# Attention of a decoder step: four score banks in a ring, and the scores issued one job ahead

## What is computed

```python
def nsa_block(qp, qb):                       # per 128 queries, 8 heads, one shared K/V
    o_c, p_c = _sdpa(qb, kc, vc, dist_c, dist_c >= 0, slopes_a)      # 32 compressed keys
    ...
    o_s, _ = _sdpa(qb[:, :, None], kg, vg, dist_s, dist_s >= 0, slopes_a)  # selected blocks
o_w = _window_banded(qn, kw[:, w_buf:], vw[:, w_buf:], slopes_a)     # the last 512 keys
...
s = jnp.einsum('bqngmd,bknmd->bngmqk', qb, kd) * (HEAD_DIM ** -0.5)  # differential, 4 heads
p = _masked_softmax(s - slopes_b * dist, dist >= 0)
a = p[:, :, :, 0] - lam * p[:, :, :, 1]
o_b = jnp.einsum('bngqk,bknv->bqngv', a, vd)
```

## Time and profile before

| what | us |
|---|---|
| median of 3 runs (2192.03 to 2200.97) | 2200.1 |
| the profiled execution, its own time | 2199.43 |
| its span, first to last instruction | 2197.6 |
| TensorE busy | 2027.6 (92%) |
| VectorE busy | 1113.2 (51%) |
| ScalarE busy | 615.8 (28%) |

### The profile page before, as it was taken

The page is one execution under the profiler, slowest core; times in us unless marked ns, Lnnn a source line. Parts: engine busy times, 40 slices in busy tenths (PEclk is TensorE's granted clock), DMA queues, the critical chain, the costliest instruction groups (busy, mean ns, idle before and its releaser), DMA issues. The chain is left out here.

```text
span 2197.6 us, 33701 instructions
## 1 busy us (share of the span) xinstructions
PE 2027.6 (92%) x12602; PEld 1823.7 (83%) x12602; DVE 1113.2 (51%) x2445; ACT 615.8 (28%) x1220; POOL 116.4 (5%) x176
## 2 busy tenths in 40 slices
PE   6989999998996899999999879699999999999997
PEld 1338888878995788888988857499999999999996
DVE  0434333333235667677766634455555555555555
ACT  2123234321222566666660021210111101111012
POOL 1021100001300000002000000000000000000000
PEclk9989999999997799999999989899999999999998
DMA  9755554321101000000003440321120111111104
GB/s 321 264 186 171 163 152 145 113 83 49 49 1 62 1 1 1 1 1 1 1 25 120 125 147 36 96 58 29 57 57 29 57 41 45 57 29 57 38 0 154
DMA packets 132537, 166.43 MB, mean 76 GB/s; under 512 B 15851, under 2 KB 98635, under 8 KB 132372
## 3 DMA queue, kind: packets, MB, share of 16 engines
q1 hardware_dynamic: 117790, 134.75, 19.3%
q0 software_dynamic: 4832, 17.15, 2.5%
q10 hardware_dynamic: 9808, 13.11, 1.7%
HBM read 144.31 MB, written 22.77 MB: 76 GB/s over the span
## 5 line engine op out<-in xcount | busy, mean ns | idle before, releaser
L1642 DVE TENSOR_TENSOR late_x<-late_x,ffn_po 128x344 f32<-128x344 f32 x528 | 244.2, 509 | 116.4 <-PE ffn_po L1572 116.1
L1555 PE MATMUL ffn_pg<-late_words_hi,ffn_uhi 128*128 128x344 f32 x528 | 169.3, 321 | 14.7 <-DVE ffn_ulo L1606 14.7
L788 PE MATMUL nsa_out<-zs_z,nsa_probT 128*128 128x64 f32 (+1 forms) x1344 | 176.1, 277 | 5.8 <-DVE zs_z L944 5.6
L1516 ACT ACTIVATE ffn_sg<-ffn_pg 128x344 f32<-128x344 f32 x66 | 30.2, 458 | 534.2 <-PE ffn_pg L1555 534.2
L788 PEld LDWEIGHTS nsa_out<-zs_z,nsa_probT 128*128 128x128 f32 x1344 | 169.1, 198 | 7.8 <-DVE zs_z L944 7.7
L1572 PE MATMUL ffn_po<-ffn_a_hi,ffn_ohi 128*128 128x344 f32 x528 | 169.0, 320 | 0.2 <-DVE late_x L1642 0.2
L1555 PE MATMUL ffn_pg<-late_words_lo,ffn_uhi 128*128 128x344 f32 x528 | 169.1, 320 | 0.0
L1555 PE MATMUL ffn_pg<-late_words_hi,ffn_ulo 128*128 128x344 f32 x528 | 169.1, 320 | 0.0
L1572 PE MATMUL ffn_po<-ffn_a_hi,ffn_olo 128*128 128x344 f32 x528 | 168.9, 320 | 0.0
L1555 PE MATMUL ffn_pv<-late_words_hi,ffn_uhi 128*128 128x344 f32 x528 | 168.8, 320 | 0.0
L1555 PE MATMUL ffn_pv<-late_words_lo,ffn_uhi 128*128 128x344 f32 x528 | 168.7, 319 | 0.0
(11 more groups left out here) (452 smaller groups left out, 4524.0 us busy)
## 6 DMA issues: line engine op xcount, KB each, us to landing
mod_wr<-in_w_ada SPq DMA_DIRECT2D x12, 2048.0 KB, 8.9
ffn_raw_u<-in_w_ffn_in SPq DMA_DIRECT2D x44, 512.0 KB, 5.8
kin_kin<-in_cache_kv SPq DMA_DIRECT2D x64, 256.0 KB, 3.5
ffn_raw_o<-in_w_ffn_out SPq DMA_DIRECT2D x22, 512.0 KB, 3.6
gate_d<-dec_gate ACTq DMA_DIRECT2D x48, 172.0 KB, 2.4
late_x<-gate_d SPq DMA_DIRECT2D x8, 1032.0 KB, 5.2
dec_raw<-in_w_in POOLq DMA_DIRECT2D x16, 512.0 KB, 5.7
dec_vin<-in_cache_kv SPq DMA_DIRECT2D x64, 128.0 KB, 2.2
```

The lines of the kernel that those rows point to most:

```text
L788: mm = pe.matmul(out[jb.group % 2][:, jb.b, 0:w], probT[t % 2][:, q, :], g.z[:, jb.k0 // P + q, at:at + w], start=(q == 0), stop=(q == til ...
L1516: act.activation(sg[(j + c) % 2][:], pg[(j + c) % 2][:, 0:TCH], ACT.Silu).then_inc(silu_done, 1)
L1555: mm = pe.matmul(bank[b][:, 0:TCH], w[j][:, v * KD + k, :], h[:, k, tok], start=(k == 0 and q == 0), stop=(k == KD - 1 and q == 2))
L1642: dve.tensor_tensor(total[:, k, tok], total[:, k, tok], po[u % 4][:, 0:TCH], ALU.add).then_inc(o_read, 1)
```

## The change

The four score banks become one tensor with a ring: an item takes as many banks as its keys need (one for up to 512 columns, two for more; every other item one), the next free ones in order, and starts again at bank 0 where it would not fit at the end. For each item the list `earlier` holds the last item that used one of its banks, and TensorE waits for that one to be drained, not for the item two back. And on TensorE `follow(x - 1)` comes after the score of job x, where `follow(x)` came: the score of a job is issued ahead of the transposes of the job five back and the products of the job six back. The programs of ScalarE and VectorE keep their order; only the places they read are others.

```diff
+    BANK, BANKS = 512, 4
+    start, earlier, at_bank, holder = [], [], 0, [None] * BANKS
+    for n, (kind, x) in enumerate(items):
+        jb = jobs[x] if kind == "unit" else jobs[x[0]] if kind == "scores" else None
+        size = (jb.k1 - jb.k0 + BANK - 1) // BANK if jb else 1
+        if at_bank + size > BANKS:
+            at_bank = 0
+        held = [holder[b] for b in range(at_bank, at_bank + size) if holder[b] is not None]
+        start.append(at_bank * BANK)
+        earlier.append(max(held) if held else None)
+        for b in range(at_bank, at_bank + size):
+            holder[b] = n
+        at_bank = (at_bank + size) % BANKS
...
-        sc = [s.ps(f"sc{i}", [P, SEQ]) for i in range(2)]
+        sc = s.ps("sc", [P, BANKS * BANK])
...
                 for n, (kind, x) in enumerate(items):
-                    slot = n % 2
-                    if n >= 2:
-                        drained(n - 2)
+                    c0 = start[n]
+                    if earlier[n] is not None:
+                        drained(earlier[n])
...
                     if kind == "unit":
                         jb = jobs[x]
-                        score(slot, 0, (qhi[jb.head % 2], qlo[jb.head % 2]), jb.tile, jb.k0, jb.k1, g.kk[jb.b]).then_inc(sc_full, 1)
-                        follow(x)
+                        score(c0, (qhi[jb.head % 2], qlo[jb.head % 2]), jb.tile, jb.k0, jb.k1, g.kk[jb.b]).then_inc(sc_full, 1)
+                        follow(x - 1)
...
                         if m == 1:
-                            follow(t)
-                for t in range(NJ, NJ + LAG + 1):
+                            follow(t - 1)
+                for t in range(NJ - 1, NJ + LAG + 1):
                     follow(t)
```

More of the change, by code:

```diff
@@ L747, in _, with score @@
             def _(pe):
-                def score(slot, c0, q, i, k0, k1, keys):
+                def score(c0, q, i, k0, k1, keys):
                     for a, b in key_chunks(k1 - k0):
                         for n in range(2):
-                            mm = pe.matmul(sc[slot][:, c0 + a:c0 + b], q[n][:, i * P:(i + 1) * P], keys[:, k0 + a:k0 + b],
+                            mm = pe.matmul(sc[:, c0 + a:c0 + b], q[n][:, i * P:(i + 1) * P], keys[:, k0 + a:k0 + b],
                                            start=(n == 0), stop=(n == 1))
@@ L821, in _ @@
                         for t in range(4):
-                            mm = pe.transpose(sc[slot][:, t * P:(t + 1) * P], qd[:, 4 * half + t].rearrange("p a b -> p (a b)"), g.ident[:])
+                            mm = pe.transpose(sc[:, c0 + t * P:c0 + (t + 1) * P], qd[:, 4 * half + t].rearrange("p a b -> p (a b)"), g.ident[:])
                         mm.then_inc(q_ps, 1)
@@ L827, in _ @@
                         for t in range(4):
-                            mm = pe.transpose(sc[slot][:, t * P:(t + 1) * P], q2d[:, 4 * half + t, y % 2].rearrange("p a b -> p (a b)"), g.ident[:])
+                            mm = pe.transpose(sc[:, c0 + t * P:c0 + (t + 1) * P], q2d[:, 4 * half + t, y % 2].rearrange("p a b -> p (a b)"), g.ident[:])
                         mm.then_inc(q2_ps, 1)
@@ L832, in _ @@
                         for i in range(TT):
-                            mm = score(slot, 32 * i, (qhi[x % 2], qlo[x % 2]), i, 0, 32, g.kkc)
+                            mm = score(c0 + 32 * i, (qhi[x % 2], qlo[x % 2]), i, 0, 32, g.kkc)
                         mm.then_inc(sc_full, 1)
@@ L837, in _ @@
                         for half in range(2):
-                            mm = pe.transpose(sc[slot][:, half * P:(half + 1) * P],
+                            mm = pe.transpose(sc[:, c0 + half * P:c0 + (half + 1) * P],
                                               scmp[:, 4 * half:4 * half + 4, :].rearrange("p t n -> p (t n)"), g.ident[:])
@@ L843, in _ @@
                         for half in range(2):
-                            mm = pe.matmul(sc[slot][:, half * 4 * HD:(half + 1) * 4 * HD], pcT[:, half, :],
+                            mm = pe.matmul(sc[:, c0 + half * 4 * HD:c0 + (half + 1) * 4 * HD], pcT[:, half, :],
                                            g.vcb[:].rearrange("p a b -> p (a b)"), start=True, stop=True)
@@ L855, in _ @@
                             pe.wait_ge(q2_lo, 4 * jb.head + 2 * m + 2)
-                        score(slot, 0, (q2hi[m], q2lo[m]), jb.tile, 0, jb.k1, g.kk[2 + jb.head // 2 * 2 + m]).then_inc(sc_full, 1)
+                        score(c0, (q2hi[m], q2lo[m]), jb.tile, 0, jb.k1, g.kk[2 + jb.head // 2 * 2 + m]).then_inc(sc_full, 1)
                         if m == 1:
-                            follow(t)
-                for t in range(NJ, NJ + LAG + 1):
+                            follow(t - 1)
+                for t in range(NJ - 1, NJ + LAG + 1):
                     follow(t)
@@ L898, in _ @@
                         act.wait_ge(q_ps, 2 * h + half + 1)
-                        act.activation(qhi[h % 2][:, half * HALF:(half + 1) * HALF], sc[n % 2][:, 0:HALF], ACT.Copy).then_inc(q_hi, 1)
+                        act.activation(qhi[h % 2][:, half * HALF:(half + 1) * HALF], sc[:, start[n]:start[n] + HALF], ACT.Copy).then_inc(q_hi, 1)
                     if kind == "two queries":
@@ L902, in _ @@
                         act.wait_ge(q2_ps, 2 * y + half + 1)
-                        act.activation(q2hi[y % 2][:, half * HALF:(half + 1) * HALF], sc[n % 2][:, 0:HALF], ACT.Copy).then_inc(q2_hi, 1)
+                        act.activation(q2hi[y % 2][:, half * HALF:(half + 1) * HALF], sc[:, start[n]:start[n] + HALF], ACT.Copy).then_inc(q2_hi, 1)
                     if kind == "unit":
@@ L1003, in minimum @@
                     dve.wait_ge(sc_full, scored[n])
-                    dve.tensor_tensor_reduce(pr, sc[n % 2][:, 0:w], table[:, -w:], -1.0, 3e38, ALU.add, ALU.min, negmax).then_inc(biased, 1)
+                    dve.tensor_tensor_reduce(pr, sc[:, start[n]:start[n] + w], table[:, -w:], -1.0, 3e38, ALU.add, ALU.min, negmax).then_inc(biased, 1)
                 def close(t):
@@ L1026, in _ @@
                 for n, (kind, x) in enumerate(items):
-                    at_sc = sc[n % 2]
+                    at_sc = sc[:, start[n]:]
                     if kind == "queries":
```

## The result

The changed kernel takes 2268.6 us (median of 4 runs) against 2200.5 us: a ratio of 1.032, 95% interval 1.029 to 1.034. It is 68 us slower. The forecast had the sign right, 16 us of it, and a range that ended at 2240 us. All of the difference is in the attention stage: the last products, issued at 1143.67 us before, are issued at 1208.85 us now, 65 us later.

A forecast was written before the change was run, and what follows sets the result against it. TensorE was taken to bound the attention stage. New stalls of 44 us, counted as 33, less 10.2, 8 and 2, gave +13 us idle; with +3 us of clock on 2199.4 us that made 2216 us, range 2180 to 2240 us.

The forecast's parts named there:

- an unmoved `close(x)`: On VectorE, `close(x)` follows the minimum of x and waits for second-group transposes of x-4, now behind score x+1; 80 jobs.
- The overlap: TensorE's new stalls: each gives VectorE and ScalarE time for the next chain, so three quarters of 44 us count, 33 us.
- the neighbours: Score banks: 6 items wait for the one directly in front, in tile 4 and differential jobs; 7.4 us together.
- the queries: TensorE: 15 items wait for an item "queries" of the job directly before; 1.6 us each, 12 counted, 19 us.
- distance three: Score ring: 89 items wait for the item three back, asking for the same minimum as before.
- The 8 us taken off for the other waits: TensorE's waits for output buffer, evacuation and minimum, 11.5 us: 8 go, since scores reach VectorE earlier.
- The 2 us off at the start: Start of the attention stage: the ring lets the first four items go at once, clock at half; 2 us off.
- The clock: TensorE's granted clock: a third more idle time brings a fifth more of the some 15 us lost, +3 us.
- every chain bites: Rival: no overlap, 44 us of stalls, the clock falls after each group; 2243 us, chance 0.10.
- So 105 items are tighter: Score items of ring distance one or two ask for a later minimum than before: 105 tighter, 89 as before, 50 looser.
- the starved engine: Rival: scoring ahead lets VectorE enter each burst a round earlier, idle 25.4 to 8 us; 2177 us, chance 0.20.
- 97 short chains: Items whose next score waits for transposes, VectorE's copy, finish and minimum; fewer than about 15 stalling favours the faster rival.

The follow-up runs named there:

- order alone, two slots: Against the kernel before: scores issued one job ahead, but with the two fixed slots of two banks instead of the ring; 2282.8 us, ratio 1.040.
- VectorE's copy later: Against the change: only VectorE's second-half copy moved one job later, ScalarE's evacuation left as it was; 2251.8 us, ratio 1.025.
- ScalarE's evacuation later: Against the change: only ScalarE's evacuation moved one job later, VectorE's second-half copy left as it was; 2229.0 us, ratio 1.013.
- copies later, scores not ahead: Against the kernel before (two slots, old order): evacuation and second-half copy both moved one job later; 2384.2 us, ratio 1.084.
- the ring alone: Against the change: TensorE's old order put back, the ring of four banks kept; 2194.8 us, ratio 0.998 to the kernel before.
- the healed order: Against the change: evacuation and second-half copy both one job later, 2183.1 us; there, banks picked by oldest holder instead of as a ring, 2183.3 us.
- all three kernels: The change, 2268.6 us; the ring with TensorE's old order, 2194.8 us; the change with evacuation and second-half copy one job later, 2183.1 us.
- the best kernel: Against the change: ScalarE's evacuation and VectorE's second-half copy both one job later; 2183.1 us, ratio 0.993 to the kernel before.

## Why the prediction was right and wrong

**The direction and the place were right.** TensorE's order against an unmoved `close(x)` was named as what makes the change cost something, the copy's wait was to rise from 0.4 us (it is 89.7), VectorE's wait for scores was to fall under 30 (18.0), the minima's wait was to rise over 12 (22.8), and the output buffer's to fall (0.6).

**The overlap was the first step that failed.** The sum of the prices, before any discount, was near: 44 us. In the stretch, the waits for minima, queries and the steps of the compressed branch are 22.8 + 0.6 + 19.2 + 3.9 + 1.8 + 1.6 + 0.9 = 51 us. Without the discount the forecast for it is 44 - 10.2 - 8 = 25.8 us of new idle time; measured are 52.4 - 25.4 = 27.0. The failed term is "I take three quarters of 44": there was nothing to take off. The reason given, that a stall gives VectorE and ScalarE time, doesn't hold where those two are in the same circle: as the timeline at 861 shows, they wait for TensorE's transposes while it waits for them. 11 us of the error are here. Of the classes, the neighbours came out as priced (8.5 us against 7.4) and so did the queries (19.2 against 19). But the sum is helped by chance: the items of distance three were held to be "as before", at no price, and five of them waited 5.8 us for minima in the stretch. The 8 us taken off for the other waits came true: of the 5.4 and 3.6 us, 0.6 and 0.9 are left, 7.5 us less, and the 2.5 us are in the new count. The 2 us off at the start did not: from 711 to 760 us TensorE was to idle less than 10.0 us, and idled 12.9, 49 us less the 36.09 us of the row:

```profile
711.00:760.00 49.00, 36.09 (x182) 31.90 (x182) 26.87 (x75) 20.46 (x50) 7.95 (x14) 0.71 0.00 1
```

The forecast's 13 us, 11 us for the discount and 5 us for the start make 29 us; measured were 29.9.

**The clock was the second step that failed, and the larger one.** It was priced at 3 us, by a proportion: "a third more idle time", so a fifth more loss. It cost 35 us, as much as the idle time itself. Idle time rose by 82% and time at half clock by 113%. From 760 us to the end of the stage the clock fell 10 times, before 3 times. A proportion to the idle time can't give this, and the other kernels say so too. What each has more than the kernel before, in TensorE's idle and busy time in its attention stage:

| kernel | idle, us | busy, us |
|---|---|---|
| the change | +29.9 | +35.2 |
| order alone, two slots | +43.8 | +36.3 |
| VectorE's copy later | +22.4 | +29.6 |
| ScalarE's evacuation later | +17.8 | +7.2 |
| copies later, scores not ahead | +84.5 | +92.5 |

Between 0.4 and 1.3 us of busy time come with each microsecond of idle time. What sets it is not shown; ScalarE's evacuation, moved alone, gives back less than half of the idle time and most of the clock. The rivals had it no better: "every chain bites" gave 34 us of idle, close to 29.9, but 10 us of clock. The rule of the Trainium skill, page "TensorE: Matmul & The Clock Gate", Part 1, that the clock falls after an idle window, read as the prediction read it (short scattered stalls leave the clock up), would have made the term nothing. The traces go against that reading: the longest wait of TensorE in the rows of the changed kernel above is 3.4 us, the minima's longest is 2.5, and 130 us ran at half clock.

**ScalarE had too small a part.** The prediction put what makes the tight items cost something on VectorE's `close`, and brought in ScalarE's evacuation only for the queries. That class it placed and priced rightly: with the evacuation moved alone, the waits for the queries are the ones that go. But in time ScalarE's tie carries more (39.6 us alone, against 16.8), mostly through the clock, and the last 29 us come back only with both ties loose. On ScalarE the exponential stands behind the evacuation, and behind that the copies of the queries and whatever waits for the probabilities.

**The ring distances cost much only together with the order.** "So 105 items are tighter" was counted for the ring and the order together. In the changed kernel 29 of the 105 stalled, and 16 of the 89 that were to be as before. With the ring alone the time is 2195 us, and 13 distances of two less in the healed order change nothing. The two neighbours inside a differential job stall in all three kernels, for 2 to 3 us together; the rest counts if the minimum is late, and it was late because of the order.

**The rival "the starved engine"** was right in its direction for another kernel: with the two copies moved, scoring ahead is worth 17 us over before. In the kernel as changed, the point that it named decided against it: 34 of the 97 short chains stalled, not fewer than 15.

## What to carry to other kernels

When one engine's program is shifted by a stage in a software pipeline, list for each other engine what it does in a round and ask which of it now waits for work that was moved back; shift that as well, or the engines can wait in a circle, in which their slack doesn't help. Shifting only those that follow was worse still (8.4% slower). On such a circle the stalls added up here, with nothing to discount. And price the clock with the stalls: here a microsecond of new idle time of TensorE took another 0.4 to 1.3 us of busy time, mostly through the clock, so give that term a wide range of its own.

## What the runs showed of the hardware

A short wait can come ahead of a fall of TensorE's clock, and a longer one need not. In the kernel before, TensorE was idle for 1.1 us of the 7 us to 770 us, in one wait, and the clock fell behind it; in the changed kernel it was idle for 1.9 us (7 - 5.14) from 857 to 864 us, and the clock stayed at 1.00 from 852 to 889 us. First the kernel before, then the change:

```profile
763.00:770.00 7.00, 5.90 (x43) 5.16 (x42) 5.61 (x16) 4.82 (x13) 0.00 (x0) 1.00 0.01 2
770.00:782.00 12.00, 12.00 (x61) 11.61 (x60) 5.32 (x15) 4.32 (x12) 0.00 (x0) 0.57 0.00 0
```

```profile
857.00:864.00 7.00, 5.14 (x30) 4.15 (x30) 5.09 (x14) 2.83 (x7) 0.00 (x0) 1.00 0.01 4
```

In the stage of the changed kernel what the clock took was as much as what the waits took (35.2 and 29.9 us). 65 us of useless products, laid ahead of places where TensorE could wait, cost only 20 us. Of the 17 us that the best kernel wins over before, TensorE's idle time gives 2.9 us, and its busy time, with the same instructions, 14.1 us.
